# Two-block transformer kernel in one core: eight expert weight slots in an unrolled loop, and merged norms and attentions in the second block

## The chip, the cores and the metric

One NeuronCore of a Trainium2 chip runs the whole program in a single launch. The metric is the device time of one execution in microseconds, lower is better.

## What is computed

Two blocks of two layers each, over 512 tokens of width 1024, all in fp32, batch 1. Cut to what matters:

```python
# first block: layer 0 = forgetting attention, layer 1 = retention, each followed by
def hier_moe(h, ...):                       # 32 experts, top 2 of the best group of 8
    gates = p_group * renormalised p_expert
    # expert e, on the rows routed to it, padded to blocks:
    y = (silu(xb @ w_gu[e][:, :512]) * (xb @ w_gu[e][:, 512:])) @ w_down[e]   # gu 1024x1024, down 512x1024
x = rms_norm(h, norm_final)
# second block: 512 latent tokens h and 256 context tokens hc, layer 0 (a and b mixers):
u  = rms_norm_2(h,  norm_g[0]) * (1 + scale)   + shift       # modulations from c and c_ctx
uc = rms_norm_2(hc, norm_g[0]) * (1 + scale_c) + shift_c
qb  = rms_norm_2(cq,  qn_g)  @ w_uq          # low-rank queries, width 384
kvb = rms_norm_2(ckv, kvn_g) @ w_ukv         # low-rank keys and values, width 256
y  = concat(window attention a of latents, full attention b of latents) * silu(z) @ out_w
yc = the same for the context's own queries, over context keys only
# layer 1: neighbourhood attention, then the last norm
```

Each expert has 6 MB of weights (two halves of `w_gu` and one `w_down`, 2 MB each), and every expert is computed: 192 MB for a layer of experts, twice.

## The kernel before

The program is a list of stages (`timeline`, `parts` at the end of `build`). On PE, DVE, ACT and POOL the function `run` (L1837) makes an engine wait at the start of stage k until all four engines have finished stage k-1 (semaphores `done_*`, waits on L1843), runs the stage's own code, drains the engine and counts itself done (L1845). `slack` lets a named engine go one stage further ahead. SP has no such barrier: it only issues weight loads, in program order, each one held back by the semaphore that says its slot is free. Everything behind a waiting load on SP waits too.

Weights live in `ring`: three slots of 2 MB (`RING`, `SLOT`). The arena is a scratch area of 26624 floats per partition that each stage divides up anew (`region`).

One moe layer is four stages: the norm `nf` with its transposes into `XT` (class Norm, L348), `Route` (router products on L813, ranking on DVE, then eight indirect scatters of the tokens' rows into `xg_dram`), `Experts` (L928) and `Combine` (L1190: eight indirect gathers from `y_dram`, then eight DVE operations on `H`, L1210).

`Experts` handles one expert per turn in 64-row blocks. ACT loads the 64 rows from `xg_dram` into `XG` (L1158 to L1165), PE turns them (`turn_x`, L1030), DVE copies them out with the gain (`take_x`, L1105), PE multiplies by the two `w_gu` halves (`up`, L1038), ACT and DVE make the hidden rows, PE multiplies the hidden rows of the expert before by `w_down` (`down`, L1051), and ACT copies the result to `Y` and stores it in two halves (L1119). There is a single `XG`, a single `XGT` and a single `Y`. Experts 0, 1, 30 and 31 are written out, 2 to 29 are a hardware loop (L976). SP loads in the order gate-up of expert e, first half and second half, then down of expert e-1, through the three ring slots; the loads wait for the semaphores `gated` (first half of `up` done), `upped` (second half) and `downed`.

After the second moe layer come `RowNorm` (writes the normed rows back to `H`, L778), two `Norm` stages `m00` and `m01` (latent and context rows, scaled and transposed into `XT`), and mixer a: `Products` pa, `Attend` aa (latents, 8 heads by 4 query tiles = 32 units) and `Attend` ac (context, 16 units), `OutProj` oa (its sum into `H` and `HC` is on POOL, L583). Mixer b: `Products` pb (L463), four `Norm` stages on the low-rank rows (L1686), and twice `Products` pb0/pb1, `Attend` ba0/ba1 (16 units of 768 keys), `Attend` bc0/bc1 (8 units of 256 keys), `OutProj`. `Attend` runs three units deep: scores of unit n, transposes (L670) of unit n-3, and the product with the values (L681) behind them. Scores sit in four PSUM banks: 4 units in flight if the window is at most 512 wide, else 2 (`depth`).

## Time and profile before

| | |
|---|---|
| runs, median of 3 (lowest to highest) | 3588.87 us (3587.87 to 3589.56) |
| the profiled execution | 3582.91 us, span 3581.1 us |
| PE busy | 2990.6 us (84%) |
| DVE, ACT, POOL busy | 835.7, 639.9, 191.2 us |
| moved over DMA | 604.45 MB, of which the weights' queue 537.15 MB |

"Busy" adds up the time in which an engine had an instruction in hand; it is an average over stages with different limits, so the stretches below matter more. A span is the time from the first to the last instruction.

### The profile page before, as it was taken

What the parts mean: (1) busy time and instruction counts of PE and PEld (TensorE: products, weight loads), DVE (VectorE), ACT (ScalarE), POOL (GpSimd) and SP (SyncE); (2) the same over time, 40 slices, a digit from 0 to 9 for tenths busy, and PEclk for the clock granted to TensorE, in tenths of its full rate; (3) what the DMA queues carried; (4) which work ended last, traced back from release to release, by engine and by line L of the source; (5) the groups of instructions that cost most, each with busy time, mean ns of one, the idle gap of its engine ahead of it and who ended that gap; (6) DMA issues with size and microseconds to landing.
All of it is one profiled execution on the core that took longest, in us unless ns stands there. A gap on an engine that the chain in (4) does not pass through costs nothing. (4 is left out here: it accounts for less than half of the span.)

```text
span 3581.1 us, 33057 instructions
## 1 busy us (share of the span) xinstructions
PE 2990.6 (84%) x12650; PEld 1489.5 (42%) x12650; DVE 835.7 (23%) x2158; ACT 639.9 (18%) x1369; POOL 191.2 (5%) x146
## 2 busy tenths in 40 slices
PE   7999858888859999995888888398879887989987
PEld 3544532222214444443222222256456454455554
DVE  1221321111111211212111110317323342053054
ACT  2211300000011000001000000216224241042043
POOL 0000010000000000001000000100100102011011
PEclk9999969898989999996989899699989988999999
DMA  5411059999984233232999999310000101120110
GB/s 200 190 48 71 26 198 394 391 394 394 394 319 158 94 118 118 94 118 79 388 391 393 395 393 394 118 41 14 13 24 25 36 24 47 47 65 24 47 42 30
DMA packets 191589, 604.45 MB, mean 169 GB/s; under 512 B 9941, under 2 KB 24218, under 8 KB 191338
## 3 DMA queue, kind: packets, MB, share of 16 engines
q1 hardware_dynamic: 165360, 537.15, 39.5%
q10 hardware_dynamic: 20858, 46.88, 4.3%
q0 software_dynamic: 5248, 18.75, 1.4%
q8 instruction: 80, 1.31, 0.2%
q14 instruction: 43, 0.35, 0.0%
HBM read 559.16 MB, written 43.52 MB: 168 GB/s over the span
## 5 line engine op out<-in xcount | busy, mean ns | idle before, releaser
L1038 PE MATMUL psum<-ring,arena 128*64 128x512 f32 x2048 | 564.1, 703 | 176.6 <-DMA ring<-in_expert_w_gu 174.7
L463 PE MATMUL psum<-ring,XT 128*128 128x512 f32 (+3 forms) x1216 | 478.5, 554 | 12.3 <-ACT arena L1598 6.6
L453 PE MATMUL psum<-XT,ring 128*128 128x512 f32 (+1 forms) x1152 | 444.2, 547 | 4.2 <-POOLq L1845 2.4
L1038 PEld LDWEIGHTS psum<-ring,arena 128*64 128x64 f32 x2048 | 159.0, 159 | 538.1 <-issue 300.4
L463 PEld LDWEIGHTS psum<-ring,XT 128*128 128x128 f32 x1216 | 229.6, 190 | 252.8 <-issue 219.6
L553 PE MATMUL psum<-ring,arena 128*128 128x512 f32 x704 | 311.2, 603 | 10.0 <-ACT arena L588 5.7
L453 PEld LDWEIGHTS psum<-XT,ring 128*128 128x128 f32 x1152 | 219.2, 191 | 228.1 <-issue 218.8
L652 PE MATMUL psum<-arena 128*128 128x512 f32 (+8 forms) x704 | 256.3, 481 | 42.0 <-ACT arena L706 33.7
L1051 PE MATMUL psum<-ring,arena 128*64 128x512 f32 x1024 | 233.8, 598 | 25.9 <-DMA ring<-in_expert_w_down 25.9
L1112 DVE TENSOR_TENSOR arena<-arena,psum 64x512 f32<-64x512 f32 x64 | 44.2, 690 | 751.6 <-ACT arena L1115 751.6
L553 PEld LDWEIGHTS psum<-ring,arena 128*128 128x128 f32 x704 | 135.2, 194 | 181.3 <-issue 167.0
L390 PE MATMUL psum<-cst,arena 128*128 128x128 f32 x254 | 49.1, 379 | 159.3 <-ACT arena L361 159.3
L652 PEld LDWEIGHTS psum<-arena 128*128 128x128 f32 (+2 forms) x704 | 120.9, 195 | 122.7 <-issue 60.2
L706 ACT ACTIVATE arena<-psum,sm 128x768 f32<-128x768 f32 (+5 forms) x224 | 158.1, 706 | 68.7 <-DVE sm L1782 39.8
L1115 ACT ACTIVATE arena<-psum 64x512 f32<-64x512 f32 x64 | 37.7, 589 | 733.4 <-PE psum L1038 733.4
L694 ACT ACTIVATE arena<-psum 128x512 f32<-128x512 f32 (+3 forms) x336 | 145.1, 467 | 100.7 <-PE psum L670 99.3
L670 PE MATMUL psum<-cst,arena 128*128 128x128 f32 x944 | 143.1, 276 | 18.7 <-DVE arena L748 9.9
L720 DVE TENSOR_REDUCE sm<-psum 128x1 f32<-128x256 f32 (+5 forms) x160 | 99.4, 622 | 176.4 <-PE psum L654 95.5
L681 PE MATMUL psum<-arena 128*64 128x128 f32 x1888 | 127.8, 279 | 7.1 <-ACT arena L694 7.1
L491 ACT ACTIVATE arena<-psum 128x512 f32<-128x512 f32 x64 | 36.5, 570 | 531.8 <-PE psum L463 366.1
L670 PEld LDWEIGHTS psum<-cst,arena 128*128 128x128 f32 x944 | 112.2, 142 | 46.2 <-DVE arena L748 24.7
L1051 PEld LDWEIGHTS psum<-ring,arena 128*64 128x64 f32 x1024 | 68.8, 136 | 148.9 <-issue 136.9
(216 smaller groups left out, 2173.2 us busy)
## 6 DMA issues: line engine op xcount, KB each, us to landing
ring<-in_expert_w_gu SPq DMA_DIRECT2D x128, 2048.0 KB, 12.2
ring<-in_expert_w_down SPq DMA_DIRECT2D x64, 2048.0 KB, 13.1
ring<-in_ada_w SPq DMA_DIRECT2D x12, 2048.0 KB, 8.1
ring<-in_fox_w_in SPq DMA_DIRECT2D x8, 2048.0 KB, 8.7
arena<-xg_dram ACTq DMA_DIRECT2D x64, 256.0 KB, 6.6
y_dram<-arena ACTq DMA_DIRECT2D x128, 128.0 KB, 5.9
ring<-in_ret_w_in SPq DMA_DIRECT2D x8, 2048.0 KB, 10.4
ring<-in_c_in_w SPq DMA_DIRECT2D x8, 2048.0 KB, 7.8
```

The costliest lines, as they stand in the source:

```text
L390: i = pe.transpose(bank(c % 8)[:, t * P:(t + 1) * P], self.scaled[:, t, c * P:(c + 1) * P], ident)
L453: i = pe.matmul(ps[0][0:cols_[1] - cols_[0], 0:ntok], w[:, c, cols_[0]:cols_[1]], x[:, c, tok:tok + ntok], start=(c == 0), stop=(c == k - 1))
L463: i = pe.matmul(ps[0][:, 0:width], x[:, c, t * P:(t + 1) * P], w[:, c, c0:c0 + width], start=(c == 0), stop=(c == k - 1))
L553: i = pe.matmul(bank(self.bank0 + n % 4), self.x[:, c, t * P:(t + 1) * P], w[:, c, half * BANK:(half + 1) * BANK], start=(c == 0), stop=(c ...
L652: i = pe.matmul(self.s_at(n, c0, c1), lhsT, rhs, start=True, stop=True)
L670: i = pe.transpose(bank(b)[:, j * P:(j + 1) * P], self.P[:, u % 4, (k0 + j) * P:(k0 + j + 1) * P], ident)
L681: ins = pe.matmul(psum[hh * DH:(hh + 1) * DH, (6 + pair % 2) * BANK + i * P:(6 + pair % 2) * BANK + (i + 1) * P], self.v(h + hh, kt), self ...
L694: act.activation(self.PT[:, m % 2, u % 2, k0:k0 + k, :], bank(b)[:, 0:k * P].rearrange("p (k q) -> p k q", k=k), ACT.Copy)\
L706: act.activation(self.P[:, n % 4, 0:hi - lo], self.s_at(n, lo, hi), ACT.Exp, bias=sm[:, 0, n:n + 1], accum_out=sm[:, 1, n:n + 1]).then_inc ...
L720: ins = dve.tensor_reduce(sm[:, 0, n:n + 1], self.s_at(n, *self.window(i)), AXX, ALU.max, negate=True)
L1038: i = pe.matmul(psum[side * BR:(side + 1) * BR, 0:FF], self.XGT[:, 4 * part + c, :], w[:, c, side * FF:(side + 1) * FF], start=(part == 0 ...
L1051: i = pe.matmul(psum[half * BR:(half + 1) * BR, 5 * BANK:6 * BANK], self.HT[:, c, :], w[:, c, half * BANK:(half + 1) * BANK], start=(c == ...
```

## The change

Experts: the ring's three slots are joined by five more in the arena (`SLOTS = 8`, `ARENA0`), the loads go in the order gate-up, gate-up, down of each expert, and unit v waits for unit v-8. Units 3 to 7 wait until all four engines have finished a named stage (`after`), in which the arena area is used for the last time; in the retention layers `R_YT` moves to the arena's start for that. The loop is written out for all 32 experts. Rows are loaded for two experts at once (128 rows, 512 KB), into two `XG` buffers, turned and copied out once per pair.

Second block: `m01` runs beside the second `Combine`. `TwoNorms` takes the place of `RowNorm` and `m00`: it multiplies `H` by the gain first, takes both sums of squares, and gets both factors by a bit-trick start and three Newton steps on DVE (`root_of`), so that ScalarE's square root and its table are not used; POOL writes `H`. The context units of each attention are appended to the latent units of the same `Attend` (`more`). The four low-rank norms run inside the stage pb (`LoraNorms`), and the gate products of the first half of b are moved there from pb0. Stages pb, pb1 and pc1 need not wait for POOL's part of the stage before.

```diff
 class Experts(Stage):
+    SLOTS = 8
+    ARENA0 = 2048 * 3
+    def weights(self, v):
+        s = v % self.SLOTS
+        w = ring[:, (self.base + s) % RING, :] if s < RING else region(self.ARENA0 + SLOT * (s - RING), SLOT)
     def sp(self, sp):
...
-                if is_at(e, 1):
-                    sp.wait_ge(*Weights.freed[self.base - 1])
-                    gu(e, 0)
-                    sp.wait_ge(self.s("gated"), 1)
...
+        for v in range(3 * NE):
+            e, what = divmod(v, 3)
+            if v < RING:
+                sp.wait_ge(*Weights.freed[self.base + v - RING])
+            elif v < self.SLOTS:
+                k = self.after(v - RING)
+                for other in done:
+                    sp.wait_ge(done[other], k + 1)
+            else:
+                sp.wait_ge(*self.used(v - self.SLOTS))
+            src = self.dn[e] if what == 2 else self.gu[e, :, 4 * what:4 * what + 4, :]
+            sp.dma_start(self.weights(v), src).then_inc(self.s(f"ready{v % self.SLOTS}"), 16)
...
+    def act(self, act):
+        rows(0)
+        rows(1)
+        for e in range(NE):
+            act.wait_ge(self.s("upped"), self.at("upped") + e + 1)
+            self.silu(act).then_inc(self.s("silu"), 1)
+            if e % 2 and e // 2 + 2 < NE // 2:
+                act.wait_ge(self.s("turned"), self.at("turned") + e // 2 + 1)
+                rows(e // 2 + 2)
+            if e:
+                result(e - 1)
...
+        def free_in_fox(i):
+            return place(("n0", "fa1", "fa1", "fa1", "fo1")[i])
+        def free_in_retention(i):
+            return place("rn3")
...
+            if layer:
+                combine.beside = Norm("m01", HC, D, NCT, ..., side=1, junk=...).inline()
...
+        class TwoNorms(Stage):
+            def dve(self, dve):
+                dve.wait_ge(self.s("gain"), 16)
+                for t in range(NT):
+                    dve.tensor_tensor(self.Z[:, t, :], H[:, t, :], self.G, ALU.mult).then_inc(self.s("weighted"), 1)
...
+                root_of(dve, *(s2[:, j, self.one] for j in (0, 2, 3, 1)))
...
+                root_of(dve, *(s2[:, j, self.two] for j in (0, 2, 3, 1)))
+                dve.tensor_tensor(s2[:, 3, self.one], r, s2[:, 1, self.two], ALU.mult).then_inc(self.s("rstd"), 1)
...
+            def pool(self, pool):
+                pool.wait_ge(self.s("rstd"), 1)
+                for t in range(NT):
+                    pool.tensor_scalar(H[:, t, :], self.Z[:, t, :], s2[:, 1, t:t + 1], None, ALU.mult)
...
-            Attend("ac", 8, NCT, lambda i: (0, CTX),
+            aa.more(8, NCT, lambda i: (0, CTX),
...
+        class LoraProducts(Products):
+            def pe(self, pe):
+                super().pe(pe)
+                self.norms.pe(pe)
...
+            uz0 = gate_unit(0)
+            use_units(p, u1, u2, uz0)
+            p.slack = {(e, "pool"): 1 for e in ("pe", "act", "dve")}
```

On SP, behind the last output weight of the forgetting attention, the expert loads stood like this (`ring` is the three-slot buffer; the last five rows are the hardware loop's body):

```order
L208 DMA ring<-in_fox_w_out 128x4x1024
L983 DMA ring<-in_expert_w_gu 128x4x1024 x4
L983 DMA ring<-in_expert_w_down 128x4x1024
L976 UNCONDITIONAL_BRANCH
L983 ISA
L983 DMA ring<-in_expert_w_gu 128x4x1024
L983 ISA
L983 DMA ring<-in_expert_w_gu 128x4x1024
```

and stand like this now (`arena` is the scratch area with the five added slots):

```order
L209 DMA ring<-in_fox_w_out 128x4x1024
L1030 DMA ring<-in_expert_w_gu 128x4x1024 x2
L1030 DMA ring<-in_expert_w_down 128x4x1024
L1030 DMA arena<-in_expert_w_gu 128x4x1024 x2
L1030 DMA arena<-in_expert_w_down 128x4x1024
L1030 DMA arena<-in_expert_w_gu 128x4x1024 x2
L1030 DMA ring<-in_expert_w_down 128x4x1024
```

Eight loads stand ahead of the first that waits for an expert's work, where three stood before.

On PE, in mixer b, from the last output product of mixer a to the first products of pb0, before (L390 are the transposes of the four norms):

```order
L553 MATMUL psum<-ring,arena 128x512 x48
L463 MATMUL psum<-ring,XT 128x384 x48
L463 MATMUL psum<-ring,XT 128x288 x48
L390 MATMUL psum<-cst,arena 128x128 x30
L463 MATMUL psum<-ring,arena 128x384 x3
L463 MATMUL psum<-ring,arena 128x512 x2
```

and now (L467 are the gate products, L1825 the transposes of the norms):

```order
L567 MATMUL psum<-ring,arena 128x512 x48
L477 MATMUL psum<-ring,XT 128x384 x48
L477 MATMUL psum<-ring,XT 128x288 x48
L467 MATMUL psum<-XT,ring 128x512 x8
L467 MATMUL psum<-XT,ring 128x256 x8
L1825 MATMUL psum<-cst,arena 128x128 x30
L477 MATMUL psum<-ring,arena 128x384 x3
```

(the pair of L467 rows stands twice there, once for each 128 columns of the gate). The gate products of pb0 moved in front of the 30 transposes.

## Rows read from the trace of the kernel before

**Rows 1.** The page: what moved in 40 slices, and the costliest groups of PE.
```profile
GB/s 200 190 48 71 26 198 394 391 394 394 394 319 158 94 118 118 94 118 79 388 391 393 395 393 394 118 41 14 13 24 25 36 24 47 47 65 24 47 42 30
L1038 PE MATMUL psum<-ring,arena 128*64 128x512 f32 x2048 | 564.1, 703 | 176.6 <-DMA ring<-in_expert_w_gu 174.7
```

**Rows 2.** Busy time in stretches: start:end, length, five engines, PE clock, DMA share, GB/s.
```profile
440.00:490.00 50.00, 20.60 (x105) 20.11 (x103) 16.79 (x91) 4.00 (x12) 7.83 (x8) 0.53 0.21 84
502.00:520.00 18.00, 16.32 (x84) 6.13 (x80) 3.19 (x5) 1.18 (x2) 0.00 (x0) 1.00 0.97 346
700.00:1000.00 300.00, 246.16 (x1044) 83.94 (x1040) 30.70 (x51) 20.16 (x34) 0.00 (x0) 0.90 1.03 394
1627.00:1660.00 33.00, 15.93 (x98) 15.61 (x98) 12.09 (x66) 12.36 (x25) 2.95 (x4) 0.64 0.20 69
```

**Rows 3.** Timeline of SP's issues around the first experts: start, length, what.
```profile
425.22 0.37 SPq L983 DMA_DIRECT2D ring<-in_expert_w_gu  x1
...
501.66 0.37 SPq L983 DMA_DIRECT2D ring<-in_expert_w_gu  x1
...
520.36 0.37 SPq L983 DMA_DIRECT2D ring<-in_expert_w_down  x1
```

**Rows 4.** Timeline of PE at the end of the first layer's experts.
```profile
1039.55 0.65 PE L1044 MATMUL psum<-cst,arena 128*128 128x128 f32 x4
1040.85 3.65 PE L1051 MATMUL psum<-ring,arena 128*64 128x512 f32 x16 [0.65 <-DMA ring<-in_expert_w_down]
```

**Rows 5.** DMA issues, time to landing: row loads, row stores, the gain.
```profile
arena<-xg_dram ACTq DMA_DIRECT2D x64, 256.0 KB, 6.6
y_dram<-arena ACTq DMA_DIRECT2D x128, 128.0 KB, 5.9
arena<-in_norm_final ACTq DMA_DIRECT2D x1, 512.0 KB, 6.8
```

**Rows 6.** Timeline from the end of Combine to the start of pa.
```profile
2265.64 5.99 SPq L208 DMA_DIRECT2D ring<-in_ab_in_w  x3
2268.39 0.38 ACTq L765 DMA_DIRECT2D arena<-in_norm_final  x1
...
2275.86 4.87 DVE L778 SCALAR_TENSOR_TENSOR H<-H,st,arena 128x1024 f32<-128x1024 f32 x4
...
2287.02 0.16 DVE L339 TENSOR_TENSOR st<-st 128x4 f32<-128x4 f32 x1
2287.22 2.19 ACT L361 ACTIVATE arena<-H,st 128x1024 f32<-128x1024 f32 x2 [0.83 <-DVE st L339]
...
2296.90 1.06 ACT L318 ACTIVATE arena<-HC 128x1024 f32<-128x1024 f32 x1 [0.67 <-DVEq L1845]
...
2306.34 13.97 PE L463 MATMUL psum<-ring,XT 128*128 128x512 f32 x32 [0.82 <-DVEq L1845]
```

**Rows 7.** Groups of POOL: its sums into `H`.
```profile
L583 POOL TENSOR_TENSOR H<-arena,H 128x512 f32<-128x512 f32 x40 | 51.1, 1278 | 736.8 <-DVE arena L575 736.8
```

**Rows 8.** PE around the four low-rank norms and the gate products of mixer a.
```profile
2383.11 41.45 PE L453 MATMUL psum<-XT,ring 128*128 128x512 f32 x128
2589.09 3.14 PE L463 MATMUL psum<-ring,XT 128*128 128x384 f32 x9 [2.39 <-POOLq L1845]
2650.61 2.79 PE L390 MATMUL psum<-cst,arena 128*128 128x128 f32 x12 [7.05 <-ACT arena L361]
2673.34 7.68 PE L463 MATMUL psum<-ring,arena 128*128 128x384 f32 x16 [0.76 <-POOLq L1845]
```

**Rows 9.** Busy time as in rows 2, context attention bc0.
```profile
2774.00:2786.00 12.00, 9.37 (x64) 5.92 (x64) 6.81 (x25) 6.88 (x24) 0.00 (x0) 1.00 0.00 0
```

**Rows 10.** PE at the seam of ba0 and bc0.
```profile
2771.55 1.53 PE L681 MATMUL psum<-arena 128*64 128x128 f32 x24 [0.80 <-ACT arena L694]
2774.12 1.97 PE L652 MATMUL psum<-arena 96*128 96x256 f32 x8 [1.04 <-POOLq L1845]
2776.67 0.44 PE L670 MATMUL psum<-cst,arena 128*128 128x128 f32 x2 [0.59 <-DVE arena L748]
```

More of the change, by code:

```diff
@@ L340, in inverse_roots, with root_of @@
             dve.wait_ge(stage.s("rstd"), stage.at("rstd") + 1)
+        def root_of(dve, ms, y, t, out):
+            dve_step.then(dve, dve.tensor_scalar(y.bitcast(U32), ms.bitcast(U32), -0.5, float(0x5F3759DF), ALU.mult, ALU.add))
+            for k in range(3):
+                dve_step.then(dve, dve.tensor_tensor(t, ms, y, ALU.mult))
+                dve_step.then(dve, dve.scalar_tensor_tensor(t, t, -0.5, y, ALU.mult, ALU.mult))
+                dve_step.then(dve, dve.scalar_tensor_tensor(out if k == 2 else y, t, 1.5, y, ALU.add, ALU.mult))
         class Norm(Stage):
@@ L602, in build, with __init__, more, window @@
             nsink = rt[:, 11, 0:8]
[L604 removed]
+            def __init__(self, tag, heads, nq, window, scores, keys, v, out, add=None, sink=False, masks_on_pe=False):
                 super().__init__(tag)
[L608 to L613 removed]
+                self.heads, self.add, self.sink, self.masks_on_pe = heads, add, sink, masks_on_pe
                 self.P = region(0, 4, 768)
                 self.PT = region(3072, 2, 2, 6, P)
[L617 to L619 removed]
+                self.parts, self.unit, self.first, self.pairs = [], [], [0], []
+                self.more(heads, nq, window, scores, keys, v, out)
+            def more(self, heads, nq, window, scores, keys, v, out):
+                self.parts.append((window, scores, keys, v, out, nq))
+                k = len(self.parts) - 1
+                for pair in range(heads // 2):
+                    self.pairs.append((k, pair, len(self.unit)))
+                    for r in range(2 * nq):
+                        self.unit.append((k, 2 * pair + r % 2, r // 2))
+                        self.first.append(self.first[-1] + (len(keys(r // 2)) + 3) // 4)
+                self.units = len(self.unit)
+                self.depth = 4 if all(self.window(n)[1] <= BANK for n in range(self.units)) else 2
+            def window(self, n):
+                k, h, i = self.unit[n]
+                return self.parts[k][0](i)
+            def keys(self, n):
+                k, h, i = self.unit[n]
+                return list(self.parts[k][2](i))
             def totals(self):
@@ L712, in maximum @@
             def maximum(self, dve, n):
-                h, i = self.at_unit(n)
-                adds = self.add(i) if self.add and not self.masks_on_pe else []
+                k, h, i = self.unit[n]
+                adds = self.add(i) if self.add and not self.masks_on_pe and k == 0 else []
                 for c0, c1, a in adds:
@@ L726, in dve @@
             def dve(self, dve):
+                ends = {(self.pairs + [(0, 0, self.units)])[p + 1][2]: p for p in range(len(self.pairs))}
                 for n in self.steps():
@@ L940, in __init__ @@
                 super().__init__(tag)
-                self.l = layer
-                self.base, self.per = len(Weights.units), list(Weights.per)
-                for v in range(3 * NE):
+                self.l, self.after = layer, after
+                self.base = len(Weights.units)
+                for v in range(RING):
                     Weights.add((0, 0, 0, None))
-                end = self.base + 3 * NE
-                Weights.freed[end - 3] = (self.s("upped"), NE)
-                Weights.freed[end - 2] = (self.s("downed"), NE - 1)
@@ new lines, in s, with totals, used @@
+            def s(self, name):
+                return sem(f"{self.tag if name[:2] == 'x_' else self.kind}_{name}")
+            def totals(self):
+                slots = {f"ready{s}": 16 * len(range(s, 3 * NE, self.SLOTS)) for s in range(self.SLOTS)}
+                return dict(slots, gated=NE, upped=NE, downed=NE, open=1, turned=NE // 2, ht=NE, y=NE, padded=1, xt=NE // 2, h=NE,
+                            h_turned=NE, silu=NE, rows0=16 * NE // 4, rows1=16 * NE // 4, stored=32 * NE)
+            def used(self, v):
+                e, what = divmod(v, 3)
+                name = ("gated", "upped", "downed")[what]
+                return self.s(name), self.at(name) + e + 1
@@ L1045, in turn_h, with down @@
                 return i
-            def down(self, pe, slot):
-                w = ring[:, slot, :].rearrange("p (k n) -> p k n", k=4)
+            def down(self, pe, w):
                 for c in range(4):
@@ L1081, in body @@
                     self.turn_h(pe).then_inc(self.s("h_turned"), 1)
-                    if last:
-                        down(e, True)
-                self.loop(pe, body)
+                down(NE - 1)
                 n = pe.value_load(ovn[0:1, 0:1], min_val=0, max_val=EXTRA)
@@ L1338, in fox, with place, moe @@
                 use_units(OutProj(f"fo{g}", u, 4, GT, NT), u)
-        def moe(layer):
+        def place(tag):
+            return next(k for k, stage in enumerate(timeline) if stage.tag == tag)
+        def free_in_fox(i):
+            return place(("n0", "fa1", "fa1", "fa1", "fo1")[i])
+        def free_in_retention(i):
+            return place("rn3")
+        def moe(layer, after):
             rows = region(0, NT, D)
@@ L1772, in maximum @@
             def maximum(self, dve, n):
[L1773 removed]
+                seg, h, i = self.unit[n]
                 if i == 0:
```

492 lines of the change are left out of this document (286 added, 206 removed).

## The prediction

> **What bounds the kernel now.** I read the page first, for where the bytes go. The 40 slices fall into two blocks that move about 394 GB/s (slices 7 to 11 and 20 to 25) and long stretches far below; in the two blocks lie the two layers of experts, and PE's dearest group, the product with `w_gu`, waited 174.7 us for its weights in all [rows 1]. The busy table by stretches then says that the experts are bound by the transfers and by nothing else: in 300 us amid the first layer's the DMA engines are full (share 1.03, 394 GB/s), while PE is busy 246 of them [rows 2]. SP's timeline gives the price of one weight unit of 2 MB. Its first load that waits for an expert's work goes out at 501.66, and the last unit has landed at 1040.85, when PE takes up the last `down` [rows 3, 4]. Of the layer's 96 units three were loaded before; so 93 took 539.2 us, **5.80 us a unit**, row loads and stores included, 17.4 us an expert. Just before, the same engines are nearly idle: 84 GB/s between 440 and 490, since all three slots are full and `up` of expert 0 hasn't begun; ahead of the second layer's, 69 GB/s [rows 2]. Outside the experts PE or a chain of small operations sets the pace, and weights are no matter (13 to 65 GB/s in most slices behind the second layer [rows 1]).
>
> **The experts.** The new order lets eight units go before the first that waits for an expert. The first three wait for ring slots as before. The other five stand on SP behind the third, and the waits on stages ended long ago; so they go out from about 426 on and need some 6 x 5.80 = 35 us, landed by 461, 40 us before 501.66. I cover them with the idle stretch of [rows 2]: it has 0.79 x 50 = 40 us of free transfer time by its share of 0.21. For the second layer the area is free once the norm `rn3` is done, ahead of the last output products, and the stretch behind those moves 69 GB/s. Each layer so takes five units out of the bound stretch: 5 x 5.80 = 29.0 us. Less three things:
> - A hole at the start. Units 8 and 9 go when the two halves of `up` of expert 0 are done, as now at 501.66; unit 10 waits for `down` of expert 0, which PE does behind `up` of expert 1, at about 516. Two units keep the engines busy for 11.6 us, to some 513, and the order on SP forbids units 11 and 12 to pass. Now that `down` comes only at 520.36, but the rate in those 18 us was 346 GB/s [rows 2, 3], a hole of 2. I take 6 us for the new start in all (2 to 9).
> - Rows come for two experts, 512 KB, before the first transposes: 2 us, twice the bytes of a load that takes 6.6 us in the thick of it [rows 5], bounds 0 and 4.
> - The tail. The last unit is `down`'s, as now, but the one before it is now the second half of `w_gu`. Landed 5.80 earlier, it is followed on PE by 3.65 of `up`, 3.65 of `down` of expert 30, 0.65 of transposes and the last `down` of 3.65 [rows 4]: 11.6 - 5.8 = 5.8 us behind the last landing and a drain, where 3.65 stood. 3 us (2 to 5).
>
> That is 29 - 11 = 18 us a layer, **36 for two**; bounds 2 x (29 - 18) = 22 and 2 x (29 - 4) = 50. In between, PE has nothing to win: its 14.2 us an expert (17.4 x 246/300) stay under the transfers'. The branch of the hardware loop goes, and pairs of row turns halve their number; both lie under the wait for weights.
>
> **Norms.** From the end of the second Combine (2268.39) to pa's start (2306.34) are 37.95 us, of which the last 9.4, from 2296.90 on, are `m01` [rows 6]. It moves beside Combine, whose DVE and ACT mostly wait for gathers. `TwoNorms` can't begin to multiply before the gain has landed, 6.8 us after its issue [rows 5], at 2275.2. Then DVE: four products of 1024 elements (1.22 each by the 4.87 for four [rows 6]), two sums of squares at the same price or a little more, and 25 small operations at a pitch of 0.20 (2287.02 to 2287.22 [rows 6]): 4.9 + 2.7 + 5.0 = 12.6, so the factors stand at 2287.9, 0.7 later than now. From there it is m00's end: rows, 32 transposes, copies, 2287.22 to 2296.90 = 9.7 [rows 6], to 2297.6. Beside it POOL writes `H`, 4 x 2 x 1.28 = 10.2 us by its sums of 512 elements [rows 7], to 2298.1. Saved 8.2. Contention between DVE and POOL isn't shown by a row of this stretch; if the two row scalings on DVE each wait for one of POOL's (2.56 us), 2 to 3 us go, so I take **7**, bounds 3 and 10.
> The Trainium skill (SBUF — State Buffer, Who interferes with whom) speaks against this part: DVE and POOL hold a shared port pair as a lock for a whole instruction, when DVE runs in its two-port mode or reads two operands from SBUF. By that the row scalings could stand behind a POOL operation; the sum would be 5 instead of 7. No run here shows it yet.
>
> **Low-rank norms.** PE's last product of pb ends at 2643.56 (2650.61 less the 7.05 of idle time) and the first of pb0 begins at 2673.34 [rows 8]: 29.8 us, in which PE only does 30 transposes, at 2.79 / 12 = 0.23 us each 7.0 us. Now ACT's and DVE's chains start inside pb and the gate products, half of mixer a's 41.45, 20.7 us [rows 8], stand in front of the transposes on PE and cover them. Those products were paid in pb0 before, so what goes is the idle time, 29.8 - 7.0 = 22.8, less a drain and the last copy, some 1.8: **21**, bounds 15 (the chain, some 22 us of small operations, outlasts the cover) and 23.
>
> **Attentions.** Context units appended to the latent units save a drain and a fill. At ba0 to bc0 the idles are 0.80 and 1.04 and, of the next units, 0.59 and a like one [rows 10], with the half-filled pipe some 4 us; twice in b, and at the wider a somewhat more by my guess, 5: 13. The context units keep their own density (9.37 of 12 us PE busy in bc0 [rows 9]) but now run two deep there, not four; if that costs 10% of two stretches of 15 us, 3. **13**, bounds 7 and 18.
>
> **POOL's sums.** Stages pb, pb1 and pc1 wait for POOL at their start: 2.39 [rows 8] against about 1.0 of a usual barrier [rows 10]: 3 x 1.35, **4**, bounds 2 and 5.
>
> Sum: 36 + 7 + 21 + 13 + 4 = **81 us**. Off the profiled execution, 3582.91, that leaves 3502; it lies 5.96 below the median of the runs, 3588.87, so the median should come at **3508**.
>
> **The rivals.**
> - *A, the sum as it stands*, 3488 to 3528. For it: the idle transfer time is there, and the idle of PE in the norms is in the rows.
> - *B, less*: the prefetch slows the routing (the router's weights and eight scatters share the engines), the start hole runs to both bounds, or the chain of the low-rank norms outlasts its cover. All at the low end, 22 + 3 + 15 + 7 + 2 = 49 us: 3540; range 3528 to 3552. Against it: the 40 us between landing and first use.
> - *C, more*: the deep queue evens out stalls between the loads also later, all terms high: 50 + 10 + 23 + 18 + 5 = 106: 3483; range 3470 to 3488. Against it: a share of 1.03 leaves nothing to even out.
> - *D, slower*: ACT's row loads and stores get stuck behind the backlog of weights. There is one `Y`; its store has 17.4 us less the copies, some 15, before the next result. Now it lands in 5.9 with at most three units queued [rows 5]. Were transfers served in order of issue, with five units ahead it would land in 5 x 5.80 + 1 = 30, each expert would take 15 longer, and 64 experts 960 us: up to 4470; it decides from a landing of 15 us on. Against it: at 2268.39 ACT's 512 KB went out beside three loads on SP, whose issue took 5.99 us, and landed in 6.8 [rows 5, 6], where three units ahead would take 17.
> - *E, the prefetch isn't one*: something holds the five loads until the experts run (the third ring slot, or the named stage). Then only the second block gains, 45: 3544.
>
> For D, DMA engines that go round-robin between the queues at packet granularity, as the Trainium skill has it (DMA: Bandwidth & Descriptors, Queues, rings and completion order), would exclude it; by that rule the sum stays 81, and the trace's 6.8 us beside three queued loads agrees.
>
> **How the numbers follow.** A has 0.66, B 0.13, C 0.11, E 0.05, D 0.04; 0.01 is left for no change by causes that I don't see. The time is A's. For eight in ten I take A and most of B's and C's near halves: 3484 to 3534. Two runs of this kernel tell 0.2%, 7 us, from nothing. Faster by over that: A, B, C, E, 0.95; within it 0.01; slower 0.04.
>
> **What the profile would show.** Eight loads on SP from about 426 on without a gap but for the queue's own, landed by 461; DMA share about 1.03 from 520 to the end of the experts, and the wait for `w_gu` down from 174.7 by about the saved 58 less holes, 140 or so. From Combine's end to pa about 30 us, not 38. No idle on PE of over 3 us between pb's products and pb0's. The context units follow the latent ones without a wait for another engine's stage. I am wrong if experts still take 17.4 us each from the first one on, if row stores land in over 15 us, or if the second block's end moves by less than 35 us against the experts' end.

## The result, and the profile after

The changed kernel takes **3466.68 us** in the median (3462.12 to 3471.9, four runs) where the kernel before took 3588.48 (four runs too, one more than shown above): a ratio of **0.9658, interval 0.9643 to 0.9673**, 122 us less. I had forecast 3508, 81 us less, in a range from 3484 to 3534. The sign was right, the time lies 17 us below the range. The profiled executions lie nearer to each other than the medians: the span went from 3581.1 to 3470.1, 111.0 us, because the one of before was some 6 us faster than its median and the one of after some 5 slower.

The page of the changed kernel, what it moved in 40 slices and the groups of PE that answer to [rows 1] (L1055 is now the product with `w_gu`, once for slots in the arena and once for the ring):

```profile
GB/s 189 213 25 76 27 250 382 411 410 411 411 309 167 73 146 106 89 98 219 321 411 411 411 411 379 121 43 15 13 38 13 61 1 48 70 46 44 29 43 31
L1055 PE MATMUL psum<-arena 128*64 128x512 f32 x1280 | 329.6, 664 | 120.4 <-DMA arena<-in_expert_w_gu 120.3
L1055 PE MATMUL psum<-ring,arena 128*64 128x512 f32 x768 | 197.2, 663 | 79.3 <-DMA ring<-in_expert_w_gu 76.5
```

This is the row that I had not foreseen: in both layers of experts the rate is **411 GB/s, not 394**. The stretches say the same (columns as in [rows 2]):

```profile
440.00:465.00 25.00, 18.82 (x96) 18.50 (x96) 6.73 (x37) 3.67 (x5) 0.00 (x0) 0.57 1.02 406
505.00:520.00 15.00, 13.58 (x60) 4.48 (x58) 1.11 (x2) 0.59 (x1) 0.00 (x0) 0.90 0.69 261
520.00:540.00 20.00, 20.00 (x100) 7.17 (x96) 3.46 (x5) 2.37 (x4) 0.00 (x0) 1.00 0.77 286
700.00:980.00 280.00, 217.20 (x946) 74.69 (x944) 29.97 (x43) 20.15 (x34) 0.00 (x0) 0.93 1.03 411
```

The first row is the early loads, at 406 GB/s until about 465 (from 465 to 490 it is 118), 37 us ahead of the first `up` at 502.32. Rows two and three are the hole at the start. The last one has the DMA share of 1.03 that [rows 2] had too, at 17 GB/s more: the share says that the engines always had something in hand, and nothing about how fast they were through with it.

Where the 111 us of span lie, from the stages' starts on PE in both traces. The experts run from the first transposes of the rows to the end of the last `down`, 493.77 to 1044.50 before and 498.96 to 1013.18 after in the first layer. Combine ends where the gain's load is issued, at 2268.39 before and 2195.99 after.

| stretch | before | after | gained | forecast |
|---|---|---|---|---|
| first layer's experts | 550.7 | 514.2 | 36.5 | 18 |
| second layer's experts | 551.8 | 512.5 | 39.3 | 18 |
| Combine's end to pa | 37.95 | 31.42 | 6.5 | 7 |
| pb's start to the first scores of ba0 | 135.0 | 108.5 | 26.5 | 21 |
| the three merged attentions to their OutProj | 239.5 | 230.5 | 9.0 | 13 |

The rest, 7 us less of a gain than these add up to, lies in stretches whose work didn't change (the program up to the first router products took 448.5 instead of 443.1; in the other kernels here the same work took 441.6 to 448.9), and in the stages' starts without POOL, which gave 1.4 us each.

The timeline of the changed kernel from the gain's arrival to pa, which answers to [rows 6] (L1614 is the product with the gain, L1631 the scaling of the rows, L1639 POOL's writing of `H`):

```profile
2203.13 4.63 DVE L1614 TENSOR_TENSOR arena<-H,arena 128x1024 f32<-128x1024 f32 x4 [7.36 <-DMA arena<-in_norm_final]
...
2215.15 2.28 DVE L1631 TENSOR_SCALAR arena<-arena,rt 128x1024 f32<-128x1024 f32 x2
2215.33 11.76 POOL L1639 TENSOR_SCALAR H<-arena,rt 128x1024 f32<-128x1024 f32 x4 [27.32 <-DVE rt L1628]
...
2227.41 4.94 PE L477 MATMUL psum<-ring,XT 128*128 128x512 f32 x7 [4.24 <-POOLq L2049]
```

POOL ends last, at 2227.09, and pa begins behind it.

PE at the low-rank norms, which answers to [rows 8] (L467 the gate products, L1825 the 30 transposes):

```profile
2554.75 7.44 PE L477 MATMUL psum<-ring,XT 128*128 128x288 f32 x30
2562.03 20.80 PE L467 MATMUL psum<-XT,ring 128*128 128x512 f32 x64
2583.30 3.50 PE L1825 MATMUL psum<-cst,arena 128*128 128x128 f32 x30 [0.47 <-ACT arena L505]
2587.72 4.54 PE L477 MATMUL psum<-ring,arena 128*128 128x384 f32 x12 [0.92 <-POOLq L2049]
```

The gap is gone, and the 30 transposes take 3.50 us in all.

### The profile page after: what moved, and what is told of

Read it like the earlier page. It is cut to its first block and busy times, and to the rows that moved or that the text cites. A ratio compares the mean times of both kernels' runs of the same rounds, so it can differ in the third digit from the quotient of the medians.

```text
span 3470.1 us, 30692 instructions
## 1 busy us (share of the span) xinstructions
PE 2919.9 (84%) x12394; PEld 1467.3 (42%) x12394; DVE 835.9 (24%) x2143; ACT 633.5 (18%) x1356; POOL 200.0 (6%) x148
## 3 DMA queue, kind: packets, MB, share of 16 engines
q10 hardware_dynamic: 20346, 46.88, 3.9%
## 5 line engine op out<-in xcount | busy, mean ns | idle before, releaser
L467 PE MATMUL psum<-XT,ring 128*128 128x512 f32 (+1 forms) x1152 | 444.1, 547 | 2.8 <-DVEq L2049 2.8
L1055 PE MATMUL psum<-arena 128*64 128x512 f32 x1280 | 329.6, 664 | 120.4 <-DMA arena<-in_expert_w_gu 120.3
L467 PEld LDWEIGHTS psum<-XT,ring 128*128 128x128 f32 x1152 | 219.7, 191 | 226.3 <-issue 215.2
L1055 PE MATMUL psum<-ring,arena 128*64 128x512 f32 x768 | 197.2, 663 | 79.3 <-DMA ring<-in_expert_w_gu 76.5
L1055 PEld LDWEIGHTS psum<-arena 128*64 128x64 f32 x1280 | 97.2, 151 | 326.1 <-issue 190.3
L734 ACT ACTIVATE arena<-psum,rt 128x768 f32<-128x768 f32 (+5 forms) x224 | 158.2, 706 | 61.7 <-DVE rt L1984 41.3
L698 PE MATMUL psum<-cst,arena 128*128 128x128 f32 x944 | 143.1, 277 | 12.5 <-DVE arena L778 8.2
L1067 PE MATMUL psum<-arena 128*64 128x512 f32 x640 | 144.9, 595 | 1.1 <-DVE arena L1122 1.1
L1055 PEld LDWEIGHTS psum<-ring,arena 128*64 128x64 f32 x768 | 59.9, 150 | 200.8 <-issue 136.5
L748 DVE TENSOR_REDUCE rt<-psum 128x1 f32<-128x256 f32 (+5 forms) x160 | 99.7, 623 | 166.5 <-PE psum L682 98.7
L505 ACT ACTIVATE arena<-psum 128x512 f32<-128x512 f32 x64 | 36.5, 570 | 531.2 <-PE psum L477 366.2
## 6 DMA issues: line engine op xcount, KB each, us to landing
arena<-in_expert_w_gu SPq DMA_DIRECT2D x80, 2048.0 KB, 25.4
```

The lines of the kernel that those rows point to most:

```text
L467: i = pe.matmul(ps[0][0:cols_[1] - cols_[0], 0:ntok], w[:, c, cols_[0]:cols_[1]], x[:, c, tok:tok + ntok], start=(c == 0), stop=(c == k - 1))
L698: i = pe.transpose(bank(b)[:, j * P:(j + 1) * P], self.P[:, u % 4, (k0 + j) * P:(k0 + j + 1) * P], ident)
L734: act.activation(self.P[:, n % 4, 0:hi - lo], self.s_at(n, lo, hi), ACT.Exp, bias=sm[:, 0, n:n + 1], accum_out=sm[:, 1, n:n + 1]).then_inc ...
L748: ins = dve.tensor_reduce(sm[:, 0, n:n + 1], self.s_at(n, *self.window(n)), AXX, ALU.max, negate=True)
L1055: i = pe.matmul(psum[side * BR:(side + 1) * BR, 0:FF], x[:, 4 * part + c, :], w[:, c, side * FF:(side + 1) * FF], start=(part == 0 and c = ...
L1067: i = pe.matmul(psum[half * BR:(half + 1) * BR, 5 * BANK:6 * BANK], self.HT[:, c, :], w[:, c, half * BANK:(half + 1) * BANK], start=(c == ...
```

## Experiments

The diffs show the lines that matter; the counts of semaphores that go with them are left out.

**Three slots, same new order** (slots3). Does the rate come from the slots?

```diff
-            SLOTS = 8
+            SLOTS = 3
```

> The changed kernel with three slots for the experts instead of eight: loop still written out, rows still loaded in pairs, order still gate-up, gate-up, down. The experts of the first layer took 550.7 us from the first transposes to the last down before and 514.2 after; the rate was 394 and is 411 GB/s. Theory 1 (the rate comes from how many transfers are queued): 394 GB/s or less, 548 to 560 us a layer, kernel some 75 us slower than the changed one, about 3545. Theory 2 (the rate comes from larger row loads or from the written-out loop): 411 GB/s stay, only the five early units go, about 514 + 5 x 5.57 - 6 = 536 us a layer, kernel about 3510.

Measured: 4168.24 us, ratio to before 1.1598 (1.1574 to 1.1622; all ratios below are to before), 252 GB/s from 700 to 980. Neither theory: the edit changed more than the number of slots. Three slots with the load order gate-up, gate-up, down lets `down` of expert e wait for the slot of `down` of e-1, which PE only does behind `up` of e, and the loads of e+1 stand behind it on SP. SP's timeline in slots3 shows it:

```profile
823.22 0.37 SPq L1030 DMA_DIRECT2D ring<-in_expert_w_down  x1
823.63 1.06 SPq L1030 DMA_DIRECT2D ring<-in_expert_w_gu  x2
```

and PE's timeline there, around the same time:

```profile
819.57 3.61 PE L1067 MATMUL psum<-ring,arena 128*64 128x512 f32 x16
823.12 0.66 PE L1061 MATMUL psum<-cst,arena 128*128 128x128 f32 x4
837.42 9.25 PE L1055 MATMUL psum<-ring,arena 128*64 128x512 f32 x32 [13.65 <-DMA ring<-in_expert_w_gu]
```

All three loads of an expert leave within 1.5 us, as soon as `down` ends at 823.2, and PE then waits 13.65 us for them: 27 us an expert. What eight slots also do is to make this order harmless.

**Three slots in the order of before** (order3), the control that slots3 should have been.

```diff
-            SLOTS = 8
+            SLOTS = 3
+            ORDER = [u for e in range(NE) for u in ((3 * e, 3 * e + 1) + ((3 * e - 1,) if e else ()))] + [3 * NE - 1]
-                    e, what = divmod(v, 3)
+                    u = self.ORDER[v]
+                    e, what = divmod(u, 3)
-                        sp.wait_ge(*self.used(v - self.SLOTS))
+                        sp.wait_ge(*self.used(self.ORDER[v - 3]))
```

> Three ring slots and the loads in the order of before (gate-up e+1 twice, then down e), no early loads beyond three, but written out and with rows in pairs; second block as changed. It takes the place of the kernel slots3, whose order made each down load wait for the down product of the expert before. Theory 4: 411 GB/s with three slots as well; experts 93 x 5.57 + some = 525 to 535 us a layer, kernel about 3505. Theory 5b (more than three slots are needed for 411): 394 GB/s and 548, kernel about 3540.

Measured: 3499.03 us, ratio 0.9751 (0.9735 to 0.9767); 410 GB/s with three slots, and from the first `up` to the last `down` 527.1 and 525.8 us, where before had 547.9 and 549.0 and the changed kernel has 510.9 and 509.2. So the rate is not a matter of slots, and the gain parts in two: 21 and 23 us a layer with no slot added, 16 to 17 for slots and early loads.

**Eight slots without the early loads** (hold).

```diff
-                        k = self.after(v - RING)
-                        for other in done:
-                            sp.wait_ge(done[other], k + 1)
+                        sp.wait_ge(self.s("gated"), self.at("gated") + 1)
```

> Eight slots as in the changed kernel, but units 3 to 7 are issued only when the first half of expert 0's product is done, so nothing more than before is loaded ahead of the experts. Theory 1 (queued transfers give the rate, and the early loads are a gain of their own): 411 GB/s, and five units more inside the stretch at 5.57 us less the start hole that goes, 514 + 28 - 6 = 536 us a layer, kernel about 44 us above the changed one, 3510. Theory 3 (the early loads are hidden or worthless, all comes from the rate): 514 us a layer, no slower.

Measured: 3509.34 us, ratio 0.978 (0.9757 to 0.9802), 411 GB/s, 530.5 and 529.2 us a layer. Against this kernel the early loads are worth 20 us a layer, against order3 16 to 17 with the slots. My 18 for them, holes and tail included, was sound. And eight slots that are filled no earlier than three are no faster than three: order3 is 3 us a layer shorter.

**At most two, or three, weight loads under way** (flight2, flight3), early loads kept.

```diff
+                    if v >= self.SLOTS:
+                        self.ready(sp, v - 2)
```

> Eight slots and the early loads stay, but from unit 8 on SP issues a load only when the load two before it has landed, so at most two weight loads are under way. Theory 1: the rate falls back to about 394 GB/s or below and the experts take some 20 us more a layer, 534 to 545. Theory 2 (row pairs or the written-out loop): 411 GB/s and 514 us as they are.

> As the kernel with two loads under way, with three allowed. Theory 1: between, 405 to 411 GB/s, 514 to 522 us a layer; if three are as good as eight, slots beyond four bring nothing but the early loads. Theory 2: 411 GB/s and 514 us.

Measured: 3472.46 and 3464.76 us in one run each; 410 and 411 GB/s, 511.4 and 512.1 us in the first layer, as with the full queue. The time to landing shows that the edit did what it says: 11 us of a `w_gu` load in flight2, 25.4 in the changed kernel, 12.2 before. Before had as many loads under way as flight2 (12.2 us to land at 5.8 a unit, 11 at 5.6) and was slower. Theory 1, the queue, is refuted.

**Rows for one expert at a time** (rows1), slots and written-out loop kept. The rows are also turned and copied out once per expert again.

```diff
-                    act.dma_start(self.XG[m % 2], self.xgp[m]).then_inc(self.s(f"rows{m % 2}"), 16)
+                    act.dma_start(self.XG[m % 2][0:BR], self.xgb[m]).then_inc(self.s(f"rows{m % 2}"), 16)
```

> The changed kernel, eight slots, early loads and written-out loop kept, but the rows are loaded, turned and copied out for one expert at a time (64 rows, 256 KB, into partitions 0 to 63, two buffers). Theory 4 (what raises the rate is the shape of the row loads: a load into 64 partitions takes as long as one of 512 KB into 128): 394 GB/s, 17.3 us an expert, the experts some 21 us longer a layer, 530 to 535, kernel about 3508. Theory 5 (the written-out loop or the slots' order raises the rate): 411 GB/s and 510 us, kernel 3467.

Measured: 3507.55 us, ratio 0.9779 (0.9762 to 0.9795), **394 GB/s** again, 534.0 and 532.1 us. So the rate hangs on how the rows are loaded, and they are 3.8% of the bytes.

**The pair in two loads of 64, or four of 32 partitions** (rows_split, rows_split4).

```diff
-                    act.dma_start(self.XG[m % 2], self.xgp[m]).then_inc(self.s(f"rows{m % 2}"), 16)
+                    for b in range(2):
+                        act.dma_start(self.XG[m % 2][b * BR:(b + 1) * BR], self.xgb[2 * m + b]).then_inc(self.s(f"rows{m % 2}"), 16)
```

> The changed kernel with each pair's rows loaded by two transfers of 64 rows, one into partitions 0 to 63 and one into 64 to 127, issued one behind the other. Theory 4a (it is the uneven load on one half of the partitions that costs): 405 to 411 GB/s, 510 to 515 us a layer, since each pair still fills both halves. Theory 4b (it is the number of transfers or their size of 256 KB): 394 GB/s, 530 us.

> The changed kernel with each pair's rows loaded by four transfers of 32 rows, 128 KB each. Two transfers of 64 rows had 394 GB/s and 530 us a layer, one of 128 rows 411 and 510. Theory 6a (a cost per transfer of about 1.4 us): two more per pair, 18.7 us an expert, 363 GB/s, near 570 us a layer. Theory 6b (it is a matter of a load below 512 KB, whatever the number): 394 GB/s, 530 us.

Measured: 3509.57 and 3501.71 us, one run each; 394 and 393 GB/s, 528.5 and 529.6 us in the first layer, 531.1 and 530.9 in the second. The stretch from 700 to 980 in rows_split, columns as in [rows 2]:

```profile
700.00:980.00 280.00, 214.47 (x905) 73.07 (x902) 27.63 (x40) 19.03 (x33) 0.00 (x0) 0.91 1.03 394
```

These rows are turned in pairs, as in the changed kernel, so the turning is not what costs in rows1. Filling both halves of the partitions by two loads doesn't help (4a falls), and four loads cost no more than two, so it is no cost per transfer (6a falls). What was left was the size of a load or the partitions that a single one covers.

**256 KB into 128 partitions** (rows_wide): each row in two halves of 2 KB in neighbouring partitions, turned by four transposes an expert instead of eight.

```diff
-                self.xgb = xg_dram.rearrange("(b p) d -> b p d", p=BR)
+                self.xgb = xg_dram.rearrange("(b p) (h n) -> b (p h) n", p=BR, h=2)
-                    act.dma_start(self.XG[m % 2][0:BR], self.xgb[m]).then_inc(self.s(f"rows{m % 2}"), 16)
+                    act.dma_start(self.XG[m % 2], self.xgb[m]).then_inc(self.s(f"rows{m % 2}"), 16)
```

> The kernel rows1 (eight slots, rows of one expert at a time, 256 KB, 394 GB/s), but each row is split in two halves of 2 KB that lie in neighbouring partitions, so that 256 KB fill 128 partitions; four transposes instead of eight, two copies out with a step of two. Theory 7a (what costs is a transfer over only 64 partitions beside weights that fill 128): 411 GB/s, 16.6 us an expert, 510 to 514 us a layer. Theory 7b (what costs is a load below 512 KB): 394 GB/s and 532.

Measured: 3461.55 us, ratio 0.9656 (0.9637 to 0.9674), 511.4 and 512.4 us. The stretch from 700 to 980, columns as in [rows 2], in rows1:

```profile
700.00:980.00 280.00, 218.26 (x968) 79.62 (x970) 28.90 (x48) 18.98 (x32) 0.00 (x0) 0.93 1.03 394
```

and in rows_wide:

```profile
700.00:980.00 280.00, 218.14 (x932) 74.72 (x930) 30.34 (x65) 19.60 (x33) 0.00 (x0) 0.94 1.03 410
```

Same bytes, same number of loads, same 256 KB each, same share of 1.03: **it is the partitions that one load covers**. Theory 7a holds for the loads. Two other differences between these kernels drop out by the packets of ACT's queue. Every row load closes with 16 small packets, whatever it covers: the changed kernel has 20346 packets there, rows_split 512 more for its 32 loads more, rows_split4 1536 more for its 96. And rows_wide sends its rows in twice as many packets of half the size, 24954 in all against 20858 in rows1, and is the faster one.

The durations of single packets between 700 and 980 in the traces show where the time goes, and why the share can't. A row packet of 4 KB took 233 ns in the kernel before, 229 in rows1, 242 in rows_split and 232 in rows_split4, but 164 in the changed kernel. The weights' packets of 4 KB slowed down beside them, to 168 ns in before, rows1 and rows_split4 and 167 in rows_split, where they took 163 in the changed kernel and in rows_wide. The share adds up packet time, so slower packets fill it just as well. From rows1 to the changed kernel the row packets' part is 1024 x 65 ns and the weights' 24832 x 5 ns, over 16 engines 4 and 8 of the 280 us: 4% together, as the rate has it, and two thirds of it fall on the weights.

**The result stored in one transfer** (stores1, on top of best below; stores_wide, on top of the changed kernel).

```diff
-                for half in range(2):
-                    act.dma_start(self.yb[b, half], self.Y[half * BR:(half + 1) * BR, :]).then_inc(finished, 16)
+                act.dma_start(self.yb[b], self.Y).then_inc(finished, 16)
```

In stores_wide the destination is laid out anew as well:

```diff
-                self.yb = y_dram.rearrange("(b p) (h n) -> b h p n", p=BR, h=2)
+                self.yb = y_dram.rearrange("(b p) (h n) -> b (p h) n", p=BR, h=2)
```

What stores_wide leaves out: the two halves of a result's row come to lie apart in `y_dram`, and the gathers of Combine don't put them together again, so its output is not the program's. Loads, gathers and products are the same in number and size.

> The kernel best with each expert's result stored by one transfer of 256 KB from 128 partitions instead of two of 128 KB from 64. Rows in pairs took 0.72 us an expert off (17.3 to 16.6) by one transfer less for two experts. Theory 6a (every small transfer beside the weights costs the engines about 1.4 us): one less per expert, 1.4 us each, rate above 440 GB/s and up to 45 us a layer, kernel 3360 to 3400, where PE (14 us an expert) begins to bound. Theory 6b (the cost lies in the row loads, in a transfer of 256 KB with rows of 4 KB, and not in a number of transfers as such): 411 GB/s, 504 us a layer, kernel 3447.

> The changed kernel, rows in pairs, with each expert's result stored by one transfer of 256 KB from 128 partitions to 128 neighbouring half rows, so that all 16 engines share it (in stores1 the first of three dimensions was 2 and it landed in 18.6 us). The halves of a row come to lie apart in the intermediate array, which the gathers do not undo. Theory 7a for stores too: the rate rises by as much again, to about 428 GB/s, 15.9 us an expert, some 490 us a layer. Theory 7c (only loads matter, the stores read SBUF): 411 GB/s and 510. Theory 7b: one transfer less, 256 KB still below 512: 411.

Measured: stores1 3735.94 us, ratio 1.0404 (1.038 to 1.0428), 317 GB/s; stores_wide 3463.5 us, ratio 0.9659 (0.9639 to 0.9679), 411 GB/s. For these stores two halves of 64 partitions or one of 128 make no difference, and their packets of 2 KB take 85 ns in either kernel: beside this stream only what is written into SBUF counts (7c). In stores1 the destination's first dimension is 2. ACT's longest wait, in its table of waits (total, times, longest):

```profile
ACT arena L1169 <- DMA y_dram<-arena: 784.4, 56, 19.6
```

ACT can't refill the only `Y` before its store has landed: a store issued at 805.53 lets ACT copy the next result at 825.02, 19.5 us later. (The 18.6 us in the expectation of stores_wide are the landing of stores1's row pairs; its page gives none for the stores.) With a store that takes longer than an expert's weights, that is the bound. This is my rival D by another cause: 19.5 is 4.5 over the threshold of some 15 that I gave it, and the first layer took 638.9 us against 504.4 in best, 4.2 more an expert. The page's row of ACT's queue has 18426 packets instead of 20346:

```profile
q10 hardware_dynamic: 18426, 46.87, 3.6%
```

1920 fewer is 30 for each of 64 experts: 32 closing packets, 16 for each of two stores, have become 2. (In stores_wide they have become 16, 19322 packets in all.) The Trainium skill has the rule (DMA: Bandwidth & Descriptors, Why a DMA increments its semaphore by 16 and not by 1): every engine that takes part closes with a descriptor of its own, and the number of engines is the largest up to 16 that divides the slowest dimension of both sides. A 2 there gives two engines, and the trace agrees by its 2 closing packets.

**The context attentions as stages of their own** (nomerge).

```diff
-            aa.more(8, NCT,
+            Attend("ac", 8, NCT,
-                ba.more(4, NCT,
+                Attend(f"bc{g}", 4, NCT,
```

> The changed kernel with the context attentions as stages of their own again. The stretches from the first scores to the first transposes of OutProj were 107.5, 64.5 and 67.5 us before and are 103.9, 64.1 and 62.6. If the merge alone did that: back to 107.5, 68 and 67.5, in all some 12 us more. If the shortfall in the first half of b (0.5 us instead of 4) is a slower clock at its start and not the merge: that stretch becomes about 4 us longer than 64.1.

Measured: 3479.26 us in one run. From attention's start to the next products it has 163.0, 103.0 and 128.3 us where the changed kernel has 159.8, 99.5 and 124.9: merging is worth **3.1, 3.5 and 3.4 us**, 10.0 in all, in the first half of b as anywhere. That before had only 0.9 us more than the changed kernel over the first half of b (100.4 against 99.5, 1.4 of it from POOL's slack) is the clock: PE at the start of ba0 before (a stretch of 16 us, columns as in [rows 2]):

```profile
2724.00:2740.00 16.00, 13.51 (x73) 8.70 (x74) 9.23 (x17) 9.29 (x19) 0.00 (x0) 1.00 0.23 67
```

and in the changed kernel:

```profile
2616.00:2632.00 16.00, 13.55 (x46) 8.32 (x48) 8.45 (x14) 8.08 (x17) 0.00 (x0) 0.79 0.16 55
```

In the same time PE did 73 matmuls at a granted clock of 1.00, and 46 at 0.79. What the fall hangs on is open, but the merging isn't it: ba0 starts at 0.79 in nomerge too, and in every other kernel here but the one before. Nor is it where the gate products stand. Ahead of ba0, PE now has 28 us of dense products, where it had 51 with the gate products in pb0; nolora, the next kernel, has the 51 back, and the same 16 us there are no better:

```profile
2644.00:2660.00 16.00, 13.59 (x44) 8.35 (x46) 8.35 (x14) 7.96 (x17) 0.00 (x0) 0.79 0.23 67
```

The second half of b has it the other way round: ba1 started at 0.79 before (48 matmuls in its first 16 us) and starts at 0.89 now (67).

**The low-rank norms as stages of their own** (nolora): pb a plain `Products`, four `Norm` stages behind it, the gate products in both of pb0 and pb1.

```diff
-            p = LoraProducts("pb")
+            p = Products("pb")
-            gates_b(p, uz0)
-            p.norms = LoraNorms("bn", p, ((CQ, cqT, V_BQ, Q_LORA), (CKV, ckvT, V_BKV, KV_LORA))).inline()
+                Norm(f"b{nm}l", rows[:, 0:NT, :], width, NT, gain_cols(at), None, dst, 0, ...)
+                Norm(f"b{nm}c", rows[:, NT:NTA, :], width, NCT, gain_cols(at), None, dst, SEQ, ...)
```

> The changed kernel with the four low-rank norms as stages of their own again and the gate products of the first half back in pb0. From pb's start to the first scores of the first half it was 135.0 us and is 108.5, 26.5 less, of which I had forecast 21. If all of it is this part: 135 again, and the first half's attention keeps its length; if part of the 26.5 is the clock of pb0 (7.68 us for its first 16 products before, 5.83 after), it is seen there again.

Measured: 3496.5 us in one run; 135.8 us from pb to ba0, 27.3 more than the changed kernel. All of the 26.5 is this part.

**Slots in the order in which they come free, and pa without POOL** (best).

```diff
+            FREED = [u for e in range(NE) for u in ((3 * e, 3 * e + 1) + ((3 * e - 1,) if e else ()))] + [3 * NE - 1]
+            SLOT_OF = list(range(8))
+            for _v in range(8, 3 * NE):
+                SLOT_OF.append(SLOT_OF[FREED[_v - 8]])
-                        sp.wait_ge(*self.used(v - self.SLOTS))
+                        sp.wait_ge(*self.used(self.FREED[v - self.SLOTS]))
-            Z, ROWS, JUNK = region(0, NT, D), region(NT * D, NT, D), region(2 * NT * D, 2, D)
+            ROWS, Z, JUNK = region(0, NT, D), region(NT * D, NT, D), region(2 * NT * D, 2, D)
             p = Products("pa")
+            p.slack = {(e, "pool"): 1 for e in ("pe", "act", "dve")}
```

> The changed kernel with two edits: a load takes the slot that PE frees next (gate-up, gate-up, down of the expert before) instead of slot v modulo 8, so the third waiting load no longer stands behind down of expert 0; and pa need not wait for POOL's writing of H (its input moved to an area that pa leaves alone). If the start hole is what the slot order costs (286 GB/s from 520 to 540 us, a loss of 6 us a layer) and the wait of 4.24 us at pa's start is POOL's: 2 x 5 + 3.5 = 13 us faster than the changed kernel, 3454. If the hole only moves: 3463.

Measured: **3446.96 us**, ratio to before 0.9605 (0.9589 to 0.9621); the experts take 504.4 and 503.7 us, 6.5 and 5.5 less than in the changed kernel, and pa starts 3.2 us before POOL ends. Its stretch from 520 to 540 (columns as in [rows 2]):

```profile
520.00:540.00 20.00, 20.00 (x98) 7.09 (x95) 1.54 (x3) 2.35 (x4) 0.00 (x0) 1.00 1.03 414
```

POOL writes `H` from 2199.70 to 2211.47 there, and PE begins pa before it is done:

```profile
2208.30 4.10 PE L477 MATMUL psum<-ring,XT 128*128 128x512 f32 x9 [1.09 <-DVEq L2054]
```

414 GB/s stand where the changed kernel had 286. The hole was the slot order, and its price the 6 us that I had put on it. This version beats both kernels.

## Why the forecast fell short

**Right.** What bounds the experts (transfers), that the time ahead of them is free for transfers, that five loads more fit in it (20 us a layer by hold, 16 to 17 by order3, against my 18), the hole behind the ninth and tenth unit (6 us, best), the norms (6.5 against 7), the attentions (10.0 by nomerge against 13), POOL's slack (1.4 us a stage against 1.35), and that ACT's rows and stores don't stand behind SP's backlog: with some 25 us of weights queued the row pairs landed in 6.8 us and the stores in 6.0.

**The step that failed** is "Rows come for two experts, 512 KB, before the first transposes: 2 us", where I saw in the row pairs a delay and nothing else, and with it the sum's "5 x 5.80": I took the price of a unit, "5.80 us a unit, row loads and stores included", as a property of the chip, though one of the things that it included was being changed. The new loads fill 128 partitions; that alone takes 0.62 to 0.72 us off an expert (rows_split and rows1 against the changed kernel: 20 and 23 us over 32 experts, means of the two layers). Two layers make 40 to 46 us of it; the experts gave 39.8 us more than their term of 36. Rows in [rows 5] held a weak hint: 256 KB took 6.6 us to land beside the weights; after, 512 KB took 6.8. The packets of the trace of before held a plain one: 233 ns for 4 KB of rows, 168 for 4 KB of weights.

**The argument that hid it** stands in rival C: "a share of 1.03 leaves nothing to even out". The share is 1.03 at 394 and at 411 GB/s alike. Rival C named 3483, the nearest of the times, by the wrong mechanism (a deeper queue that evens out stalls between loads): with two loads under way instead of five, flight2 has 410 GB/s as well. The measured time lies below C's range too.

The Trainium skill would have told it (SBUF — State Buffer, Door 1: The DMA port swizzle): partitions 0 to 63 lie behind 8 of the 16 ports by which DMA reaches SBUF, no more than 0 to 31 do. The Trainium skill adds (SBUF — State Buffer, "Can I just issue two DMAs to hit both halves?") that two transfers to the two halves don't add up to one over all 128. By the asymptotes of the Trainium skill in the first of these sections, 218 and 436 GB/s, 256 KB would take 1.20 us on 8 ports and 0.60 on 16, an estimate of 0.60 us an expert. Measured against the changed kernel were 0.72 (rows1) and 0.62 (rows_split); rows_split4, with loads of 32 partitions, has 393 GB/s like the loads of 64, and rows_wide 410. Stores_wide shows that it didn't matter for reading SBUF here. The runs show which loads are slow; that ports are why is the word of the Trainium skill, no run here sees a port.

**A term mis-sized:** the low-rank norms, 21 forecast, 26.5 measured, 27.3 by nolora. I let the 30 transposes stay at the 7.0 us of [rows 8]. But there PE was idle three quarters of the time and its clock was granted at 0.54 (the trace from 2644 to 2673), close to the lower level of 1.2 GHz. Behind the gate products, at 1.00, they take 3.50. Then pb0 starts warm too: its first 16 products take 5.83 us, where the last row of [rows 8] has 7.68.

**A sign that did not come:** I expected the waits for `w_gu` to fall from 174.7 to 140 us. They rose to 196.8, while those for `w_down` (25.9 before) all but went; the sum hardly moved. From the first `up` to the last `down` of both layers the time fell by 77 us, 1096.9 to 1020.0, but PE's busy time fell as much, 895.4 to 819.2, since half of the row transposes are gone and the clock was 0.93 instead of 0.90. A sum of waits is no measure of what a change gained.

**DVE and POOL in the norms.** I had left 2 to 3 us open for contention. The two row scalings took 2.28 us beside POOL, where `m00`'s took 1.42 (in the trace of before, from 2287.22), 0.9 more; and POOL's four took 11.76, not 10.2, and ended last. All of the 0.9 is in the second scaling: it began at 2215.82 and took 1.61 us instead of 0.75, and it ended 1.2 us before POOL's first operation did (2215.33 to 2218.63). That two such operations slow each other agrees with the rule that I weighed (the Trainium skill, SBUF — State Buffer, Who interferes with whom); that the other one is blocked for the whole instruction does not, as the second scaling would then have ended behind 2218.63. The sum by it, 5, was further from the 6.5 than the 7. No run here took POOL's work away, so that a shared port is the cause is not shown.

## What to carry to other kernels

When a stretch is bound by transfers, its price per unit is made of everything that is on the queues, the small transfers too; ask of each edit whether it changes one of them, its partitions above all, before the old price is multiplied. Here 3.8% of the bytes, sent to 64 partitions, cost 4% of the rate, and the same 256 KB laid over 128 partitions cost nothing. A DMA share of 1 says that the engines are occupied, not that they are at their best; and slots are to be handed on in the order in which they come free, or a first-in-first-out queue of loads stands still behind the one that is not.

## What the runs showed that I had not expected

- The rate beside small loads: 394 GB/s when rows go to 64 or 32 partitions, whether in one, two or four transfers; 410 or 411 when one transfer goes to 128, of 256 or of 512 KB.
- A packet of 4 KB for a load into 64 or 32 partitions took 229 to 242 ns, into 128 partitions 164; the weights' own packets went from 163 to 168 ns beside the former.
- Two weight loads of 2 MB under way keep the engines as busy as five do: 410 against 411 GB/s.
- A store of 256 KB whose destination has 2 as its first dimension held up the next result for 19.5 us; with 128 as its first dimension it landed in 6.1.
- The granted clock at the start of an attention differs for the same work, 0.79 or 1.00 at ba0: 46 instead of 73 matmuls in 16 us. It hid 3.5 us that the merging gains there, and it fell with and without the merging.
